# Values first at the attention's entry: side steps moved to the retention, the first pair's projection ahead of the fourth value slab

## What is computed

```python
    for i in range(DEPTH):
        m_lat = jnp.split(cond_lat @ ada_w[i] + ada_b[i], 6, axis=-1)
        m_ctx = jnp.split(cond_ctx @ ada_w[i] + ada_b[i], 6, axis=-1)
        a_lat = modulate(h_lat, m_lat[0], m_lat[1])
        a_ctx = modulate(h_ctx, m_ctx[0], m_ctx[1])
...
        h_lat = layer_norm(DEEPNORM_ALPHA * h_lat + m_lat[2] * y_lat, ln_g[i, 0], ln_b[i, 0])
        f_lat = swiglu(modulate(h_lat, m_lat[3], m_lat[4]), ffn_w13[i], ffn_w2[i])
        h_lat = layer_norm(DEEPNORM_ALPHA * h_lat + m_lat[5] * f_lat, ln_g[i, 1], ln_b[i, 1])
```

## Time and profile before

| | |
|---|---|
| median of 3 runs | 3174.45 us (3172.67 to 3175.84) |
| the profiled execution | 3191.96 us, span 3190.7 us |
| TensorE matmul busy | 3049.1 us (96% of the span) |
| VectorE busy | 2014.7 us (63%) |
| ScalarE busy | 1233.4 us (39%) |
| side steps on VectorE at L565 (main group) | 187.3 us in 215 instructions of mixed forms |

### The profile page before, as it was taken

One profiled execution on the slowest core, in us unless ns is written; L12 is line 12 of the kernel. 1 busy time (PEld: TensorE's weight loads), 2 busy tenths in 40 slices (PEclk: granted clock), 3 DMA queues, 4 the chain that ended last, 5 costly groups with the idle time before them and its releaser, 6 DMA issues.

```text
span 3190.7 us, 55249 instructions
## 1 busy us (share of the span) xinstructions
PE 3049.1 (96%) x23638; PEld 2868.9 (90%) x23638; DVE 2014.7 (63%) x2878; ACT 1233.4 (39%) x1633; POOL 340.1 (11%) x331
## 2 busy tenths in 40 slices
PE   7999998999998799998999999999999999999999
PEld 4888887999998677998999989889999998997998
DVE  4576586777786577677656854566565576446654
ACT  2222223545443133433544421445454443134643
POOL 5000001101010122002100020011020102000201
PEclk9999998999998799898998989999999999999999
DMA  7243244799996566797655612346576663232664
GB/s 262 95 151 127 89 156 116 204 258 270 262 280 196 160 210 201 202 257 215 180 164 151 168 54 67 100 131 180 169 197 168 168 160 92 65 96 69 191 168 129
DMA packets 746224, 524.76 MB, mean 164 GB/s; under 512 B 19242, under 2 KB 711660, under 8 KB 745852
## 3 DMA queue, kind: packets, MB, share of 16 engines
q1 hardware_dynamic: 741852, 516.18, 56.4%
q0 software_dynamic: 4128, 5.06, 0.5%
HBM read 520.07 MB, written 2.94 MB: 164 GB/s over the span
## 4 chain that ended last, share of the span: by engine, by line
PE 79%; DVE 9%; ACT 5%; issue 5%; DMA 2%; SPq 0%; POOL 0%; DVEq 0%; ACTq 0%; POOLq 0%
PE bank L478 21%; PE bank L479 20%; PE bank L480 20%; ACT weights_hi L448 3%; PE bank L1415 2%; PE bank L596 2%; DVE weights_lo L458 1%; DVE conv_out L2242 1%; PE bank L2407 1%; PE bank L820 1%; PE bank L2419 1%; PE bank L2415 1%; DMA side_weights<-in_ada_w 1%; PE bank L1420 1%; DVE side_sums_odd L565 1%
## 5 line engine op out<-in xcount | busy, mean ns | idle before, releaser
L458 DVE TENSOR_TENSOR weights_lo<-weights_raw,weights_hi 128x2048 fp32r<-128x2048 f32 (+3 forms) x414 | 853.9, 2063 | 375.7 <-ACT weights_hi L448 375.2
L448 ACT ACTIVATE weights_hi<-weights_raw 128x2048 fp32r<-128x2048 f32 (+3 forms) x414 | 709.4, 1714 | 695.5 <-PE bank L480 581.6
L478 PE MATMUL bank<-ffn_in_hi,weights_hi 128*128 128x256 f32 x1184 | 344.0, 291 | 25.6 <-DVE modulation L612 16.4
L479 PE MATMUL bank<-ffn_in_lo,weights_hi 128*128 128x256 f32 x1184 | 339.9, 287 | 0.0
L480 PE MATMUL bank<-ffn_in_hi,weights_lo 128*128 128x256 f32 x1184 | 339.6, 287 | 0.0
L478 PE MATMUL bank<-mix_in_hi,weights_hi 128*128 128x256 f32 x960 | 285.2, 297 | 6.2 <-DVE mix_in_lo L1926 3.7
L478 PE MATMUL bank<-mac_in_hi,weights_hi 128*128 128x256 f32 x1024 | 289.5, 283 | 1.5 <-DVE mac_prod L2025 1.0
L480 PE MATMUL bank<-mac_in_hi,weights_lo 128*128 128x256 f32 x1024 | 289.8, 283 | 0.0
L479 PE MATMUL bank<-mac_in_lo,weights_hi 128*128 128x256 f32 x1024 | 289.5, 283 | 0.0
L479 PE MATMUL bank<-mix_in_lo,weights_hi 128*128 128x256 f32 x960 | 277.4, 289 | 0.0
L480 PE MATMUL bank<-mix_in_hi,weights_lo 128*128 128x256 f32 x960 | 277.0, 289 | 0.0
(11 more groups left out here) (442 smaller groups left out, 7487.7 us busy)
## 6 DMA issues: line engine op xcount, KB each, us to landing
weights_raw<-in_ffn_w SPq DMA_DIRECT2D x132, 512.0 KB, 6.4
weights_raw<-in_w_in SPq DMA_DIRECT2D x120, 512.0 KB, 5.0
side_weights<-in_ada_w SPq DMA_DIRECT2D x85, 576.0 KB, 4.4
weights_raw<-in_ffn_wg SPq DMA_DIRECT2D x88, 512.0 KB, 4.0
weights_raw<-in_ffn_wu SPq DMA_DIRECT2D x88, 512.0 KB, 5.3
weights_raw<-in_ffn_wd SPq DMA_DIRECT2D x64, 704.0 KB, 4.6
weights_raw<-in_ffn_w SPq DMA_DIRECT2D x48, 704.0 KB, 6.7
side_weights_third<-in_ada_w SPq DMA_DIRECT2D x43, 576.0 KB, 4.5
```

What stands on the lines that cost most here:

```text
L448: k.s.activation(k.w_hi[s % HIGHS][:, 0:n], k.raw[s % RING][:, 0:n], ACT.Copy).then_inc(*k.hi.up())
L458: k.v.tensor_tensor(k.w_lo[s % RING][:, 0:n], k.raw[s % RING][:, 0:n], k.w_hi[s % HIGHS][:, 0:n].bitcast(F32), ALU.subtract).then_inc(*k.l ...
L478: k.te.matmul(out, l[0], r[0], start=first, stop=False)
L479: k.te.matmul(out, l[0], r[1], start=False, stop=False)
```

## The change

- Side steps. The plan has four new blocks (12 to 15) of 512 columns in place of the first two of 1024: 32 steps of 512 columns and one conditioning vector, and 16 steps of 1024 columns instead of 32. In all there are 272 steps, before 256. The retention does 128 of them, before 96: `RET_ROOM` deals them out by cost (a step for two vectors 2, for one vector 1). The attention does 48, before 64: at its value slabs 1, 2, 2, 3 instead of 2, 6, 8, 8, in the pairs 5 each as before. The feed-forward stages do as many steps as before, each of them four blocks; those in the first of them are now two blocks of 1024 and two of 1152 columns, before four of 1024.
- In the attention's entry VectorE copies a value slab first and does the side steps after it; no block is finished between value slabs.
- The slab of the first pair of heads goes ahead of the fourth value slab, and TensorE projects the first pair before that slab's values. ScalarE's copy of k and VectorE's scaling of q move with it; the turns are renumbered by `shift`, and the finish in pair 0 waits for the fourth value slab's copy.

```diff
-SIDE_M2 = 16
+SIDE_RET = 16
+SIDE_M2 = 18
-NA_V_SIDES = [2, 6, 8, 8]
+NA_V_SIDES = [1, 2, 2, 3]
-NA_FINISH = {0: 2, 2: 3, 4: 4, 5: 5, 7: 6}
+NA_FINISH = {0: 0, 2: 1, 4: 2, 5: 3, 7: 4}
...
-RET_SIDES = [1] + ([3, 3, 4, 4, 3, 1, 2, 1, 2, 1] * 4)[:30] + [4, 4, 5, 5, 3, 1, 1, 0, 0]
+RET_ROOM = [2] + [7, 7, 9, 11, 9, 3, 4, 4, 4, 4] * 3 + [5, 5, 6, 6, 6, 4, 3, 1, 0]
+def ret_sides():
+    costs = [2] * (SIDE_TWO * KD) + [1] * ((SIDE_RET - SIDE_TWO) * KD)
+    out, i, room = [], 0, 0
+    for n in RET_ROOM:
+        room, first = room + n, i
+        while i < len(costs) and costs[i] <= room:
+            room -= costs[i]
+            i += 1
+        out.append(i - first)
...
+RET_FINISH = [[b for b in range(SIDE_RET) if sum(RET_SIDES[:g - 1]) < KD * (b + 1) <= sum(RET_SIDES[:g])]
+              for g in range(len(RET_SLABS))]
...
+    slabs += values[:3] + heads[:1] + values[3:] + heads[1:]
...
+    for b in range(SIDE_RET - SIDE_TWO):
+        steps += [(a["ada_w"][1], i, 2 * D + b * SIDE1, SIDE1, (0,)) for i in range(KD)]
+    for b in range(SIDE_M2 - SIDE_RET):
+        steps += [(a["ada_w"][1], i, 4 * D + b * SIDE_WIDE, SIDE_WIDE, (0,)) for i in range(KD)]
...
+        if n == 0 and m.na:
+            te.wait_ge(k.ev.h, k.pairs0 + 2)
...
     for i in range(2, 4):
+        if i == 3:
+            pe_first_pair(k, m)
         w = pe_slab(k)
...
-        pe_side_finish(k, m.block + i - 2)
...
+        if j == 3:
+            dve_project(k, m, 0)
+        v.wait_ge(*k.used.at(j + 1 + (j > 2)))
...
+        for _ in range(NA_V_SIDES[j]):
+            dve_side(k)
```

More of the change, by code:

```diff
@@ L152 @@
 RET_SLABS = retention_order()
-RET_SIDES = [1] + ([3, 3, 4, 4, 3, 1, 2, 1, 2, 1] * 4)[:30] + [4, 4, 5, 5, 3, 1, 1, 0, 0]
-RET_FINISH = {next(g for g in range(len(RET_SLABS)) if sum(RET_SIDES[:g + 1]) >= KD * (b + 1)) + 1: b
-              for b in range(SIDE_TWO)}
+RET_ROOM = [2] + [7, 7, 9, 11, 9, 3, 4, 4, 4, 4] * 3 + [5, 5, 6, 6, 6, 4, 3, 1, 0]
[8 more added lines that the diff above has]
+        out.append(i - first)
+    assert i == len(costs)
+    return out
+RET_SIDES = ret_sides()
+RET_FINISH = [[b for b in range(SIDE_RET) if sum(RET_SIDES[:g - 1]) < KD * (b + 1) <= sum(RET_SIDES[:g])]
+              for g in range(len(RET_SLABS))]
 def wv(ap):
@@ L199, in weight_slabs @@
     wq, wn = wv(a["na_w_qkv"]), wv(a["na_w_out"])
-    slabs += [[cols(wq, i * T + 2 * D, T)] for i in range(4)]
-    slabs += [[cols(wq, n * P, P), cols(wq, n * P + D, P)] for n in range(NA_H // 2)]
+    values = [[cols(wq, i * T + 2 * D, T)] for i in range(4)]
+    heads = [[cols(wq, n * P, P), cols(wq, n * P + D, P)] for n in range(NA_H // 2)]
+    slabs += values[:3] + heads[:1] + values[3:] + heads[1:]
     slabs += [[cols(wn, i * T, T)] for i in range(4)]
@@ L869, in pe_retention @@
             pe_ret_spread(k, hd)
-        if g in RET_FINISH:
-            pe_side_finish(k, RET_FINISH[g])
+        for b in RET_FINISH[g]:
+            pe_side_finish(k, b)
 def act_ret_decay(k, hd):
@@ L1014, in dve_retention @@
                 dve_ret_taken(k, hd, c)
-                if c < sides:
+                for _ in range((sides + 3 - c) // 4):
                     dve_side(k)
@@ L1464, in pe_pairs @@
         pe_project_k(k, m, *at, half)
+def pe_pairs(k, m):
+    te = k.te
+    if not m.na:
+        pe_first_pair(k, m)
     for n in range(m.pairs):
@@ L1495, in act_project @@
     bank = k.GB[m.turn(k, n, "project") % 2]
-    k.s.wait_ge(*k.used.at(m.first + n + 1 + k.pair_slab0))
+    k.s.wait_ge(*k.used.at(m.first + n + (n > 0 or not m.na) + k.pair_slab0))
     w = 2 * T if m.na else T
@@ L1502, in act_pairs @@
     s = k.s
-    act_project(k, m, 0)
+    if not m.na:
+        act_project(k, m, 0)
     for n in range(m.pairs):
@@ L1671, in act_na @@
         act_ln_into(k, 3, k.hb[:, 1, :, :], k.am[1], n)
-    for _ in range(4):
+    for j in range(4):
         act_hi(k)
+        if j == 3:
+            act_project(k, m, 0)
     act_pairs(k, m)
@@ L1696, in dve_na @@
             dve_lo(k)
-            for _ in range(NA_V_SIDES[j]):
-                dve_side(k)
-        v.wait_ge(*k.used.at(j + 1))
-        turn = k.t0 + j
-        bank = k.GB[turn % 2]
+        if j == 3:
+            dve_project(k, m, 0)
+        v.wait_ge(*k.used.at(j + 1 + (j > 2)))
+        bank = k.GB[(k.t0 + j + (j > 2)) % 2]
         for c in range(2):
@@ L1704, in dve_na @@
                           bank[c][:, :].rearrange("p (a n) -> p a n", a=2)).then_inc(*(k.ev if c else k.dve).up())
-        if j == 0:
-            for _ in range(NA_V_SIDES[0]):
-                dve_side(k)
-        if j > 1:
-            dve_side_finish(k, m.block + j - 2)
+        for _ in range(NA_V_SIDES[j]):
+            dve_side(k)
     dve_pairs(k, m)
@@ L1727, in dve_na @@
         if i == 1:
-            dve_side_finish(k, m.block + 7)
+            dve_side_finish(k, m.block + 5)
 def block_one(k):
@@ L1802, in block_one @@
     k.pair_pt = k.hid.rearrange("p (e s) t -> p e s t", e=2)
-    pairs = Pairs(k, "na", NA_H // 2, SIDE_TWO + 8)
-    k.pairs0, k.pair_slab0 = k.t0 + 4, 0
+    pairs = Pairs(k, "na", NA_H // 2, SIDE_RET + 8)
+    k.pairs0, k.pair_slab0 = k.t0 + 3, 0
     sp_na(k)
```

36 lines of the change are left out of this document (18 added, 18 removed).

## The result

The changed kernel took 3155.69 us in the median of 5 runs (3153.69 to 3156.47), the kernel before 3175.84 (3172.67 to 3183.09) beside it: a ratio of 0.9941, 95% interval 0.9922 to 0.996. It is faster, by 20 us and not by the 34.1 of the forecast, and 3155.69 lies outside the range, which ended at 3152.

The account below looks back on a forecast made before the run. VectorE's queue of side steps was taken to pace the attention's entry, making TensorE wait. A gain of 40.5 us there, less 3.7 and 2.7 in the retention, gave 34.1 off 3174.45: 3140.3 us, range 3132 to 3152.

Parts of the forecast that it names:

- Entry, 35.1 for the projection and the values: Attention's entry: without waits and at full pace, pair 0's keys begin 20.1 us after the third value slab, 35.1 earlier.
- Pair 0 took 1097.1 - 1067.38 = 29.7 ... I give it 23.3: 6.4 less: Attention, keys of pair 0 to keys of pair 1: takes 23.3 us like pair 2, 6.4 less than traced.
- The lag of the maxima, 1.0: Attention, pair 0: three steps ahead of the maxima make VectorE late, mostly hidden; costs 1.0 us, bounds 0 and 4.1.
- Four finishes, 3.7: Retention: four added block finishes of four matmuls each on TensorE cost 3.7 us, lower bound 0.
- VectorE in the retention, 0: Retention, first three heads: seven more steps each fit into VectorE's idle time; cost 0, upper bound 6 us.
- the finish before the values "changes nothing": Retention: three finishes stand right before a head's values before and after, so waiting for VectorE's bias there changes nothing.
- The retention's end, 2.7: Last head's o0: four one-vector steps and block 15's bias delay the norm's sums by 2.7 us, bounds 1.0 and 4.6.
- Feed-forward stages, 0: Latent feed-forward stage: sixteen transfers growing from 512 to 576 KB cost 0.
- I take the difference to stay: Whole kernel: the profiled execution's 17.5 us above the median was expected to remain after the change.
- VectorE paces the retention: Rival, 0.13: half of the retention's 21 added steps are uncovered, giving back 15 us: 3155; if all, 3172.
- Slower: Rival, 0.04: retention slabs come late behind side transfers in SyncE's queue; at 1.1 us a slab, 10 slower: 3184.

Follow-up runs that it names:

- late_pair: Changed kernel with the first pair's projection and its slab put back behind the fourth value slab; 3154.3 us, 0.9926 of the kernel before.
- steps_first: late_pair with VectorE's side steps ahead of the copy again at value slabs 2 to 4; 3155.16 us, 0.9942 of the kernel before.
- early_finish: Changed kernel, retention steps dealt so no finish stands right before a head's values, last head's output slabs keeping steps; 3136.13 us, 0.9882 of the kernel before.
- quiet_end: Changed kernel, one more two-vector step in k turns of heads 0 to 2, none in the last head's output slabs; 3134.84 us, again 3129.05.
- empty_end: Changed kernel, last head's output-slab steps moved to its q, k, v and g turns, earlier heads unchanged; 3146.43 us, 0.9907 of the kernel before.
- copies_first: Kernel before with one edit: at the attention's value slabs VectorE copies first, then does its 2, 6, 8, 8 steps; 3171.72 us, 0.9987.
- after_again: Changed kernel, unchanged, timed and traced a second time; 3153.66 us, 0.9934 of the kernel before.

## Why the prediction was wrong

- **Entry, 35.1 for the projection and the values:** right. Keys 19.8 us after the third slab's end, no wait on the way. In all traces of before, S to the keys of pair 0 took 99.5, 95.5 and 98.3 us, here 64.5 and 63.3: a gain of 34 on the mean. But its reasons were only partly right: fewer steps and the missing finishes did it, in shares that no run tells apart, and the projection's new place and the copies' order add nothing that shows (late_pair, steps_first).
- **"Pair 0 took 1097.1 - 1067.38 = 29.7 ... I give it 23.3: 6.4 less":** the step that failed first, and the largest. The changed kernel did take 23.4, but the kernel before takes 23.4 and 21.8 in its other traces. The row was read as a stretch of the kernel at a low clock that the waits ahead of it cause; it was this execution's alone among the three. The term is worth 1.6 on the mean of the three traces (25.0 - 23.4), not 6.4.
- **The lag of the maxima, 1.0:** between its bounds; the maxima began 5.7 us after the keys (1051.42 against 1045.73), and pair 0 still took 23.4 us.
- **Four finishes, 3.7:** right. From its first matmul to the next one behind it, less the wait in between, each of the four takes 0.95, 0.95, 0.81 and 0.95 us in the changed kernel (from 486.26, 519.80, 532.02 and 549.66).
- **VectorE in the retention, 0, and the finish before the values "changes nothing":** wrong by 2.3 us in waits (5.0 against 3.6, and 3.1 against 2.2), within the bound of 6. That three finishes stand before values both before and after was right; what the three places cost in the clock, 5 to 7 us in either kernel, was not seen.
- **The retention's end, 2.7, upper bound 4.6:** 4.9 in the wait alone (7.83 against 2.94). The four steps at o0 took 4.1 us (529.82 to 533.92, 4.6 in the sum), but the sum stopped there: three steps at o1 took 3.5 (538.07 to 541.59) where one of 1.4 had been, and one at o2 1.2 (from 547.82) where there was none. With 4.1 less the 1.4 of before and its idle 1.18, or 1.5, at o0, that is 1.5 + 2.1 + 1.2 = 4.8, and VectorE has no idle time there to take it back. That these steps cause the wait is shown: early_finish keeps them and waits 7.4, quiet_end and empty_end have none and wait 2.7. The sum also slipped in its own terms: 548.4 and 2.0 are 550.4, and with the bias 3.0 us late, not 2.7. Together the retention is 10.0 us longer (558.1 against 548.1 on the means), the sum had 6.4; 3.7 + 4.9 + 2.3 are 10.9.
- **Feed-forward stages, 0:** not told apart. 420.6 us in the three traces of before and 423.3 in the two after, but 423.9 in copies_first, which has the steps of before, and 420.5 and 420.9 in two with the steps of after.
- **"The profiled execution took 3191.96 us at a span of 3190.7, 17.5 above the median of the runs; I take the difference to stay":** the step behind the first error. An execution that is 17.5 us above its median has those us somewhere, and the forecast took its terms from it. The difference did not stay: the changed kernel's profiled execution lay on its median.

By the means of the traces the terms are 34 + 1.6 at the entry (122.7 - 87.3 = 35.4 on the table), less 10.0 in the retention: 25 us. Against the 34.1 of the sum that is 4.8 less in pair 0, 3.6 in the retention and 1 at the projection, and 1 more for the maxima. The medians of two sessions differ by 20.2 and 20.1. The remaining 5 us stay open (the three traced executions of before average 3179.9 us, 4 above the median of the 77): three traces of one kernel that spread over 23 us don't resolve them, and the stages that the change leaves alone differ by 2 to 5 us in either direction.

Of the rivals, "VectorE paces the retention" (0.13, 3155) gave the time by luck: it gives back 15 us more there, and 3.6 were given back; the rest of its distance from the forecast is pair 0's term and the part left open. It has some of the mechanism, since VectorE's steps did pace the retention's end. "Slower" was far off: VectorE's wait for high parts in the retention did not grow from the 2.2 us of before (1.4 us), and TensorE has no wait for weights there.

## What to carry to other kernels

Look at how far the profiled execution lies from the median before taking any duration from it, and where it lies well above, distrust first those rows whose clock is low: ask for a second trace of the same kernel, or take the row's work at full clock as the other bound. When work is moved off a waiting place, count per step what hides its transfer: halving the instructions of a step while its transfer stays the same turns hidden transfers into waits, though whether those cost time depends on what the other engines do meanwhile (quiet_end has 13.2 us of them and no long wait of TensorE). A short dependent pair (a few one-column matmuls, a 0.2 us addition, then the next matmul) between two large stages cost its wait and mostly as much again or more in the clock; one slab earlier it cost neither. Look for such places in the kernel that you start from: here they were in it all along, and early_finish without them takes 17.5 us less than after_again, nearly as much as the change itself gave.

## What was unexpected of the hardware

- The time of an execution follows the mean granted clock: 3161.5 us at 0.962, 3187.9 at 0.953 for one kernel on one core in one session.
- Behind a wait of 1.28 us TensorE's values ran partly at the lower level of 1.2 GHz, which cost another 1.5 us, behind one of 2.02 it cost 3.1 (3.75 us for the first eight matmuls, which take 1.89 at full clock, and 13.6 instead of 10.5 for the 48). The loss in the clock was larger than the wait. In the second trace of the changed kernel the same wait of 2.02 us cost nothing behind it (1.96 us for the eight), so one place differs from execution to execution.
- The Trainium skill, "TensorE: Matmul & The Clock Gate", section "What's actually happening", says that the number of slow matmuls at a kernel's start varies between runs of one kernel. The traces show the like in its middle: 29.7 us at 0.71 against 23.4 at 0.93 for the same 139 matmuls of pair 0.
- The same code before the norm's sums took 543.2, 547.6, 548.3 and 548.3 us in four traces: below 5 us a single pair of traces decides nothing.
